# Splitting the modulation into a third and the rest, and moving half of the input projection into a token-major linear attention, in a three-block fp32 kernel

## The reference, cut to what matters

```python
sh1, sc1, g1, sh2, sc2, g2 = split(silu(c) @ w_ada + b_ada, 6)      # modulation of x, 6 x 1024
csh1, csc1, ... = split(silu(c_ctx) @ w_ada + b_ada, 6)             # the same for the context
hc = rms_norm(ctx, norm_mix) * (1 + csc1) + csh1                    # 256 context tokens
zf_f, zf_b, i_c = split(hc @ w_in[:, 512:2048])
s_f, s_b = hgrn2_context_states(zf_f, zf_b, i_c, lb_f, lb_b)        # states a head starts from
hx = rms_norm(x, norm_mix) * (1 + sc1) + sh1                        # 512 tokens
q, zf_f, zf_b, i, g, gate_b, gate_c, v = split(hx @ w_in)           # 8 parts of 512 = 32 tiles of 128 columns
f = lb + (1 - lb) * sigmoid(zf); k = 1 - f                          # per direction
# per head (4) and direction (2), chunks of 32 tokens, cum = cumsum(log f) inside a chunk:
scores = tril((q * exp(cum)) @ (k * exp(-cum)).T)
kv_n   = (k * exp(last - cum)).T @ v;  s_{n+1} = exp(last) * s_n + kv_n      # 16 chunks, in order
o      = scores @ v + (q * exp(cum)) @ s_n                                   # summed over directions
o = rms_norm(o, gain) * silu(g)
y = gate_b * dwconv3(gate_c * v)                                    # along rows of 64 tokens
x = x + g1 * (concat(o, y) @ w_out)
hx2 = rms_norm(x, norm_ffn) * (1 + sc2) + sh2
x = x + g2 * expert_choice_ffn(hx2)                                 # 16 experts, 64 tokens each
```

## Time and profile before

| what | us |
|---|---|
| median of 3 runs | 3802.21 |
| lowest and highest | 3798.5, 3802.88 |
| the profiled execution's own time | 3799.94 |
| its span | 3798.2 |
| PE busy in the span | 3452.6 (91%) |
| DVE busy | 1184.3 (31%) |
| ACT busy | 544.5 (14%) |
| mean granted TensorE clock | 0.932 |

### The profile page before, as it was taken

One profiled execution on the slowest core, in us unless ns is written; L12 is line 12 of the kernel. 1 busy time (PEld: TensorE's weight loads), 2 busy tenths in 40 slices (PEclk: granted clock), 3 DMA queues, 4 the chain that ended last, 5 costly groups with the idle time before them and its releaser, 6 DMA issues.

```text
span 3798.2 us, 32467 instructions
## 1 busy us (share of the span) xinstructions
PE 3452.6 (91%) x13222; PEld 1891.1 (50%) x13222; DVE 1184.3 (31%) x2278; ACT 544.5 (14%) x979; POOL 1.4 (0%) x6
## 2 busy tenths in 40 slices
PE   6999778799999999999779889999979998999998
PEld 3455554333333333358369637874434443458643
DVE  1112642311111111143564134430324099254201
ACT  1001321000000100021422031000223101020000
POOL 0000000000000000000000000000000000000000
PEclk9999668899999999999769599999998999999999
DMA  9111001699999999942000012222110121222120
GB/s 370 67 67 45 1 0 67 248 424 427 429 428 428 428 428 429 429 189 77 1 1 1 1 66 78 83 84 89 69 67 17 72 72 61 76 80 83 72 78 33
DMA packets 40935, 585.09 MB, mean 154 GB/s; under 512 B 4544, under 2 KB 4544, under 8 KB 5248
## 3 DMA queue, kind: packets, MB, share of 16 engines
q1 hardware_dynamic: 40608, 582.45, 37.7%
q0 software_dynamic: 224, 1.18, 0.1%
HBM read 581.51 MB, written 2.10 MB: 154 GB/s over the span
## 4 chain that ended last, share of the span: by engine, by line
PE 77%; DVE 11%; DMA 8%; ACT 3%; issue 1%; SPq 0%; DVEq 0%; ACTq 0%
PE PS L203 21%; PE PS L298 14%; PE PS L899 11%; DMA ring<-in_weights 7%; PE PS L506 6%; DVE A L1982 4%; PE PS L884 3%; PE PS L238 3%; PE PS L839 2%; PE PS L1616 2%; PE PS L1317 2%; PE PS L871 2%; PE PS L825 1%; PE PS L1604 1%; PE PS L512 1%; PE PS L641 1%
## 5 line engine op out<-in xcount | busy, mean ns | idle before, releaser
L203 PE MATMUL PS<-A,ring 128*128 128x512 f32 x1608 | 701.8, 599 | 39.1 <-DVE A L1953 11.8
L203 PEld LDWEIGHTS PS<-A,ring 128*128 128x128 f32 x1608 | 308.5, 192 | 431.7 <-issue 386.6
L899 PE MATMUL PS<-ring,A 128*64 128x512 f32 x2048 | 467.7, 598 | 5.0 <-DMA ring<-in_weights 3.1
L899 PEld LDWEIGHTS PS<-ring,A 128*64 128x64 f32 x2048 | 135.6, 136 | 282.8 <-issue 261.8
L884 PE MATMUL PS<-ring,A 128*64 128x512 f32 x1024 | 233.8, 598 | 27.1 <-DMA ring<-in_weights 26.8
L506 PE MATMUL PS<-H,ring 128*128 128x512 f32 x512 | 238.2, 598 | 15.2 <-DVE A L1062 15.2
L298 PE MATMUL PS<-A 128*128 128x256 f32 x1056 | 235.1, 379 | 0.0
L203 PE MATMUL PS<-H,ring 128*128 128x512 f32 x544 | 233.8, 592 | 0.0
L298 PEld LDWEIGHTS PS<-A 128*128 128x128 f32 x1056 | 200.6, 190 | 27.3
L956 DVE TENSOR_TENSOR A<-A,PS 64x512 f32<-64x512 f32 x64 | 44.1, 690 | 423.6 <-ACT A L928 423.6
L203 PEld LDWEIGHTS PS<-H,ring 128*128 128x128 f32 x544 | 103.4, 190 | 130.1 <-issue 130.1
(11 more groups left out here) (387 smaller groups left out, 3513.6 us busy)
## 6 DMA issues: line engine op xcount, KB each, us to landing
ring<-in_weights SPq DMA_DIRECT2D x274, 2048.0 KB, 9.6
X<-in_x SPq DMA_DIRECT2D x1, 2048.0 KB, 12.4
out_y<-X SPq DMA_DIRECT2D x4, 512.0 KB, 2.7
con<-in_const SPq DMA_DIRECT2D x1, 1423.0 KB, 8.0
vec<-in_vec SPq DMA_DIRECT2D x1, 1083.0 KB, 5.1
A<-in_ctx SPq DMA_DIRECT2D x1, 1024.0 KB, 14.4
con<-in_levels POOLq DMA_DIRECT2D x1, 896.0 KB, 9.0
A<-in_pos POOLq DMA_DIRECT2D x1, 256.0 KB, 4.2
```

Source lines behind the costliest of these rows:

```text
L203: mm = nc.tensor.matmul(bank[:, 0:out_width], weight_tile(name, n), moving(k), start=k == 0, stop=k == k_tiles - 1)
L899: mm = nc.tensor.matmul(PS[CAP * up:CAP * (up + 1), c % 2, :], XS[:, k, CAP * b:CAP * (b + 1)], w[:, n:n + 4, :].rearrange("p a b -> p (a ...
```

## The change

- `w_ada` is laid out in 24 units of 256 columns (half a chunk each), and one unit is 16 matmuls with 128 moving columns each. Units 0 to 7 (shift and scale of the first norm) stay at the start, as 4 chunks. Units 8 to 15 go one by one into linear attention, units 16 to 19 after its last state unit, and units 20 to 23 behind the router, while VectorE does the top-k.
- VectorE multiplies x and the context by 1/rms before the modulation is known, and later applies gain and shift in one pass, tile by tile; TensorE starts the projection with the first tile.
- The projection keeps 16 tiles (gates and values for x and the context, then q). The other 16 (g and the three parts of the convolution) are "late" products, two per chunk: pair 0 runs before the context states, pairs 1 to 7 are cut into four pieces each and laid between the steps of the units 0 to 6 of linear attention.
- Linear attention becomes token-major. `keys_values` reads 32-row slices of keys and values, so the masked copies `VB` are gone. The outputs have tokens as rows: `within` (scores times values) and `across` (queries as the 32-column stationary side, states as 128 moving columns). The head's squares are summed by ScalarE's `accum_out`, and the normed output is turned back by a transpose. One KI, KE and KET buffer is left in place of two, and QD has two in place of four.
- The convolution on VectorE is laid behind units 2, 3 and 5 and after the last.
- `vec` is loaded in two DMAs, the 16 columns that the modulation needs first.

```diff
-    ("ada", 48, 8, 0),
-    ("win1", 32, 8, 44),
+    ("ada", 16, 8, 0),
+    ("win1", 16, 8, 28),
+    ("mix1", 32, 8, 0),
+    ("ada_s", 8, 8, 0),
     ("wout1", 8, 8, 8),
+    ("ada_g", 8, 8, 0),
-ORDER1 = [*range(20, 32), *range(4, 16), *range(4), *range(16, 20)]
+ORDER1 = [*range(4, 16), *range(4)]
+LATE1 = [(16, 17), (24, 28), (20, 25), (29, 21), (26, 30), (22, 18), (27, 31), (23, 19)]
...
+        def ada_unit(pe, n, bank, name, tile0):
+            for k in range(8):
+                for half in range(2):
+                    mm = nc.tensor.matmul(PS[64 * half:64 * half + 2, bank, 0:P], SILU_C[:, k, :],
+                                          weight_tile(name, tile0 + 2 * k + half), start=k == 0, stop=k == 7)
...
+            mm.then_inc(S["ada"], 1)
...
+        def late_product(pe, c, j, ks):
+            for k in ks:
+                if k == 0:
+                    if c == 0:
+                        drained(pe, "win1", 24 + j)
+                    elif j == 0:
+                        pe.wait_ge(S["mod"], mods(7 + c))
+                    else:
+                        pe.wait_ge(S["late_out"], 2 * c)
+                mm = nc.tensor.matmul(PS[:, j, :], weight_tile("mix1", c * WT + 8 * j + k), H[:, k, :],
+                                      start=k == 0, stop=k == 7)
...
+        def late_unit(pe, c):
+            pe.wait_ge(S["late_out"], 2 * c + 1)
+            ada_unit(pe, 8 + c, 0, "mix1", c * WT + 16)
...
+            def keys_values(u):
+                if u:
+                    pe.wait_ge(S["kv_used"], u)
+                for g in range(TT):
+                    tt = tile_at(u, g)
+                    for c in range(4):
+                        rows = slice(CHUNK1 * c, CHUNK1 * (c + 1))
+                        mm = nc.tensor.matmul(PS[:, 3 + c, tt * P:(tt + 1) * P], KET[rows, tt * P:(tt + 1) * P],
+                                              VT(u // 2)[rows, tt * P:(tt + 1) * P], start=True, stop=True)
+                mm.then_inc(S["kv"], 1)
...
+            def across(u, g):
+                tt = tile_at(u, g)
+                pe.wait_ge(S["sgroup"], 4 * u + g + 1)
+                for m in range(4 * g, 4 * g + 4):
+                    n = chunk_at(u, m)
+                    c = n % 4
+                    mm = nc.tensor.matmul(PS[CHUNK1 * c:CHUNK1 * (c + 1), 2, tt * P:(tt + 1) * P],
+                                          QD[u % 2][:, n * CHUNK1:(n + 1) * CHUNK1], ST[g][:, m % 4 * P:(m % 4 + 1) * P],
+                                          start=False, stop=True, skip_group_check=True)
...
+            for u in range(8):                       # TensorE; u < 7 shown, u == 7 has units 16 and 17 instead
+                keys(u)
+                late_product(pe, u + 1, 0, range(4))
+                scores(u)
+                late_product(pe, u + 1, 0, range(4, 8))
+                keys_values(u)
+                within(u)
+                late_product(pe, u + 1, 1, range(4))
+                across(u, 0)
+                late_product(pe, u + 1, 1, range(4, 8))
+                across(u, 1)
+                output_turn(h - 1) or values(h + 1)  # one of them in a unit
+                late_unit(pe, u + 1)
+                across(u, 2)
+                pe.wait_ge(S["late_out"], 2 * u + 4)
+                ada_turn(pe, 9 + u, 0)
+                across(u, 3)
+            ada_unit(pe, 18, 0, "ada_s", 32)
+            ada_unit(pe, 19, 1, "ada_s", 48)
...
+            for u in range(8):                       # VectorE, cut in the same way
+                output_copy(h - 1)                   # every second unit, as output_scaled and output_done
+                gates_dve(dve, u + 1)
+                masked_scores(u)
+                running_sums_dve(dve, u + 1)
+                states(u, 0)
+                states(u, 1)
+                decayed_dve(dve, u + 1)
+                output_scaled(h - 1)
+                states(u, 2)
+                output_done(h - 1, turn) or values_dve(dve, h + 1, turn)
+                ada_rows_dve(dve, 9 + u, 0)
+                states(u, 3)
+                ada_mod_dve(dve, 9 + u, 1, 0)
+                if u in CONV_AT:
+                    convolution_dve(dve, CONV_AT[u])
...
             for dst, src, r in ((H, X, RX), (HC, CX, RC)):
                 dve.wait_ge(S["rstd"], S.next("dve", "rstd"))
                 for k in range(8):
+                    v = nc.vector.tensor_tensor(dst[:, k, :], src[:, k, :], r, ALU.mult)
...
+            for k in range(8):
+                for w, dst in enumerate((H, HC)):
+                    v = nc.vector.tensor_scalar(dst[:, k, :], dst[:, k, :], GM[:, k, w:w + 1], MOD[:, k, w:w + 1],
+                                                ALU.mult, ALU.add)
                 v.then_inc(S["h_ready"], 1)
```

More of the change, by code:

```diff
@@ L471, in first_tensor @@
             norm_sum(pe, lambda k: HC[:, k, :], 8, PS[:, 6, 0:TC])
[L474 to L481, removed]
             pe.wait_ge(S["silu_c"], 1)
-            for n in range(12):
+            for n in range(8):
                 if n >= 2:
                     pe.wait_ge(S["ada_rows"], n - 1)
[L487 to L493, removed]
+                ada_unit(pe, n, n % 2, "ada", 16 * n)
                 if n:
[L495 to L499, removed]
+                    ada_turn(pe, n - 1, 2, 2 * (n - 1))
+            ada_turn(pe, 7, 2, 14)
+            base, e = S.next("pe", "h_ready", 8) - 8, 0
+            pe.wait_ge(S["mod"], 1)
             for n, f in enumerate(ORDER1):
@@ new lines, in ada_turn, with ada_rows_dve @@
+        def ada_turn(pe, n, bank, col=P):
+            pe.wait_ge(S["ada_rows"], n + 1)
+            for half in range(2):
+                rows = slice(64 * half, 64 * half + 2)
+                mm = nc.tensor.matmul(PS[:, bank + half, col:col + 2], MROW(n)[rows, :], ident[rows, rows],
+                                      start=True, stop=True)
+            mm.then_inc(S["ada_turned"], 1)
+        def ada_rows_dve(dve, n, bank):
+            dve.wait_ge(S["ada"], n + 1)
+            if n >= 4:
+                dve.wait_ge(S["ada_turned"], n - 3)
+            for half in range(2):
+                rows = slice(64 * half, 64 * half + 2)
+                v = nc.vector.tensor_copy(MROW(n)[rows, :], PS[rows, bank, 0:P])
+            v.then_inc(S["ada_rows"], 1)
@@ new lines, in ada_mod_dve @@
+        def ada_mod_dve(dve, n0, units, bank, col=P):
+            dve.wait_ge(S["ada_turned"], n0 + units)
+            mod = MOD[:, 2 * n0:2 * (n0 + units), :].rearrange("p (n h) w -> p n h w", h=2)
+            bias = vcol("b_ada", 2 * n0, 2 * units).rearrange("p (n h) -> p n h", h=2)
+            for half in range(2):
+                v = nc.vector.tensor_tensor(mod[:, :, half],
+                                            PS[:, bank + half, col:col + 2 * units].rearrange("p (n w) -> p n w", w=2),
+                                            bias[:, :, half].unsqueeze(2).to_broadcast([P, units, 2]), ALU.add)
+            v.then_inc(S["mod"], 1)
@@ new lines, in keys_values, with within @@
+                mm.then_inc(S["kv"], 1)
+            def within(u):
+                h, d = u // 2, u % 2
+                pe.wait_ge(S["scores_out"], u + 1)
+                if d == 0 and h:
+                    pe.wait_ge(S["o_tok"], 2 * h - 1)
+                for tt in range(TT):
+                    s = slice(tt * P, (tt + 1) * P)
+                    nc.tensor.matmul(PS[:, 2, s], SC(h, d)[:, s], VT(h)[:, s], start=d == tt == 0, stop=True,
+                                     skip_group_check=True)
```

492 lines of the change are left out of this document (280 added, 212 removed).

## The result

The changed kernel takes 3659.01 us (median of 4 runs, 3658.74 to 3663.09); the kernel before, beside it, took 3802.49 (4 runs, 3798.5 to 3802.88). The ratio is 0.9627, with a 95% interval of 0.9611 to 0.9644: 143.5 us less. The forecast was 3686 with 3666 at its low end, so the time lies 27 us under the forecast and 7 us outside the range. The sign and the mechanism were right and the size was short.

What follows compares the result with a forecast made beforehand. Linear attention was taken as bound by no engine, TensorE and VectorE taking turns; the experts as DMA bound. From the profiled 3799.94: -116.6 + 3 - 2 = 3684.3; the median lies 2.3 higher, so 3686 us, range 3666 to 3726.

Steps and rivals of the forecast that it cites:

- low end: Whole kernel: 3666 us, reached if split tiles in linear attention cost their cheapest prices, 20 us less.
- last unit and tail: End of linear attention: 17.5 us for the last unit with two modulation units, 11 for the tail.
- clock (forecast for all stages): Waits of 4 to 6 us around 39 to 43 us and in the tail: 3 us added.
- behind the router: Four modulation units hidden in the 20.47 us top-k wait; a warmer clock may shorten the gather: -2 us.
- TensorE per unit: Linear attention loop: full-clock sum of TensorE's work in one unit, 25.4 us; with waits a unit is 26.5.
- The bound of 1.8: `keys_values` in linear attention: low end 1.8 us per unit if slices in different rows overlap; 3.4 was taken.
- across, modulation unit and turn: Linear attention, per unit: `across` 2.1 us from a 1.8 to 3.4 span, modulation unit with turn 2.4.
- mode changes: Linear attention: about 12 changes between full and split stationary tiles per unit at 0.1 us each, 1.2 us.
- The opening: Start to projection: square sums still end at 29.3 us, unit 4 waits about 4, projection starts near 56.5, not 103.8.
- Low clock in the loop (1, 3): Linear attention: 1, mean clock 0.75, 3750 us, chance 0.09; 3, 1.2 GHz throughout, slower than before, 3873, chance 0.04.
- The chain of states as the pace (2): Linear attention: state chain and waits between engines set the pace, 31 us a unit, 3720 us, chance 0.13.
- Nothing overlaps (4): Linear attention keeps its 190 us and the moved work comes on top: 16 us won, 3786 us, chance 0.04.

Runs made afterwards that it cites:

- Experiment 1: Changed kernel with the `keys_values` loops swapped, so that neighbouring matmuls read the same 32 rows: 3672.60 us, ratio 0.9662.
- experiment 3: Changed kernel with all `across` products put in the first 32 PSUM rows, output incomplete, same instructions: 3667.87 us, ratio 0.965.
- experiment 2: Changed kernel with the loops of a modulation unit swapped, its two column halves one after the other: 3680.69 us, ratio 0.9681.
- experiment 6: Changed kernel with VectorE's sixteen 1/rms passes spread between the row copies of units 0 to 5: 3652.69 us, ratio 0.9615.
- experiment 4: Changed kernel with late pairs 1 to 7 and modulation units 9 to 15 put ahead of linear attention, back to back: 3740.36 us, ratio 0.984.
- 9: Changed kernel with 1/rms passes spread, convolutions behind units 2, 4 and 6, and the output projection begun with the ready heads: 3643.18 us, ratio 0.959.

## Why the prediction was wrong in its size

By its own steps, in the profiled executions:

| step | forecast | measured |
|---|---|---|
| projection starts | 56.5 | 57.8 |
| linear attention starts | 236 | 235.8 |
| seven units | 185.5 (26.5 each) | 164.7 (23.0; two of 25.2) |
| last unit and tail | 28.5 | 25.9 |
| output projection starts | 450 | 426.4 |
| earlier than before | 116.6 | 140.2 |
| clock (forecast for all stages) | +3 | +1.9 from there to the top-k |
| behind the router | -2 | +0.3 |
| experts and the rest | 0 | -3.1 |

The +1.9: the output projection's matmuls take 58.0 us instead of 56.8 and a product of the router 5.8 instead of 5.2, the same work with some of its matmuls at a lower clock. The last row: the experts take 947.4 us from their first matmul (L1063) to the second block's first matmul, against 948.3, and what follows 2150.1 against 2152.3. Executions of one kernel differ by more than these 3.1 us.

**The step that failed** is "TensorE per unit" in linear attention, its price for small split matmuls. A unit was put at 25.4 us of TensorE work and 1.1 of waiting; the timeline of unit 2 above gives 21.78 and 1.23. Term by term, each a distance between starts:

- keys_values: 3.4 forecast, 1.10 measured, 2.3 less. The nearest row had been one of 64 rows whose instructions are also of another size, and its reading was carried to 32 rows with neighbours in different row groups, which no row of before showed. Experiment 1 measures 2.75 us without the overlap: of the 2.3, 1.65 are overlap, and 0.65 are that even the slow order was put too dear. The bound of 1.8 below was not low enough either, since it supposed the overlap of two halves where there are four groups.
- across, modulation unit and turn: 4.5 forecast, 3.6 measured. `across` is 44 ns an instruction by experiment 3's side, not the 67 of eight tiny ones; a modulation unit is 57 ns an instruction (experiment 2), which was the other of the two readings that the prediction held against each other. It took the dearer one, read from eight instructions of another kind.
- mode changes: 1.2 forecast as a term. Late products are 14.12 instead of 13.73, transposes, scores and `within` 2.98 instead of 2.60; if all of this 0.77 is laid to changes, it is less than forecast. An eight-piece of late product takes 3.43 us between full-size neighbours and 3.53 or 3.63 next to split ones.

The four make -2.3 - 0.9 - 1.2 + 0.8 = -3.6 of work a unit, and with waits of +0.1 the 3.5 by which 23.0 differs from 26.5. Seven such units are 24.5; the two with a late convolution gave 4.3 back, and the shorter first unit took 0.7: 20.8, and 2.6 more in the last unit with the tail. With the 0.2 by which linear attention began earlier, that is the 23.6 us by which the output projection came earlier than forecast. The low end had allowed 20 for cheap split tiles. Behind it, 3.1 us less in the experts and the rest, 1.1 less of lost clock, and 2.3 more behind the router make up the difference of the profiled execution, 3658.74 against 3684.3.

The rule that in the Trainium skill ("TensorE: Matmul & The Clock Gate", Part 3) lets matmuls in different row groups run at once was given 13 us in the prediction, in the low end and not in the sum; experiment 1 agrees with it, at 34 against 86 ns. Of the drain that "TensorEngine Tiling (Array Packing)", section "Key Properties", puts on a change of tiling mode, nothing over 0.1 us a change is seen: the 0.21 that the prediction weighed would be another 10 us in all, and is not there.

**What held.** The opening: a wait of 4.72 us in front of unit 4, forecast at about 4, and experiment 6 confirms the reason given. Its start did not hold: the square sums begin at 17.59 us and the modulation at 30.85 where both were put at no change (16.60 and 29.32), and in other runs the modulation began at 30.1 to 31.5. That is the 1.3 us by which the projection starts late (the forecast's own terms add to 56.1, not 56.5). The projection's end: the first late product starts at 209.16, forecast 209.3. The context's keys beside late pair 0: linear attention within 0.3 us. VectorE as the engine that orders the loop without bounding it: 14.4 us busy in unit 2 and 14.7 on average (102.9 / 7), 15.7 forecast.

**What did not hold beside that.** The -2 us for a warmer gather: TensorE idles 9.97 us ahead of the top-k's matmul, and the gather takes 9.04 us instead of 8.76. The wait of ScalarE in two units, which was not in the working: there VectorE is behind with the convolution, on top of the output copy of a head. And the last unit took 13.0 us to its last `across`, not 17.5, while its tail took 12.9 and not 11, since its two modulation units ran at half clock.

**The rivals.** Low clock in the loop (1, 3): not seen, PEclk 1.00. The chain of states as the pace (2): not seen, 0.67 us of waiting a unit; experiment 4 shows it is what would come without the late products. Nothing overlaps (4): experiment 4 is close to that kernel and takes 3740, not 3786, mostly because its linear attention with the tail takes 152.1 us and not the 190.1 that the rival kept.

## What to carry to other kernels

Price a group of small matmuls by the distance between starts of neighbours that lie as its own will: in different row or column groups they overlapped here, in the same (and in the same PSUM bank or rows) they cost 1.7 to 2.8 times as much, and the order of two loops decided it. A chain on another engine that made TensorE wait in small pieces cost twice here, by the idle time and by the clock; dense independent products in those gaps took away both (granted clock 1.00 for 0.60). Where a forecast puts many small unknown terms on the dear side at once, its low end has to hold them all at the cheap side, and below the nearest row when the geometry differs from it.

## What the runs showed of the hardware

- fp32, 128 moving columns, clock 1.00: 34 ns from start to start in four row groups of 32 rows (86 in one), 44 in four column groups of 32 (124 in one), 57 in two column halves with 2 columns each (99 in one).
- After a wait of 4.72 us the next 32 instructions took 3.58 instead of 1.92 us, so 1.2 GHz (granted clock 0.64 in the window). After waits of 1.88 us the clock sometimes stayed and sometimes did not: in the changed kernel the two units with such a wait are 2.15 us longer, while one of the two is 3.8 longer in experiment 1 (28.46 against 24.65) and in experiment 6 (26.83 against 23.01). What decides that is open.
- With the opening's wait gone (experiments 6 and 9), the projection's first matmuls ran at 1.2 GHz behind a wait of 2.1 us for a DMA. From its start to the first late product the projection took 154.2 and 153.0 us where the changed kernel takes 151.4, so this cost 2.8 and 1.6 us.
